# Retention scores: the sixteen-key tile with high and low keys in one 48-column stationary block

## The reference

```python
q, k = rotary(h @ w_q), rotary(h @ w_k) / sqrt(256)      # 4 heads, 256 wide each
s[i, j] = (q[i] . k[j]) * gamma_h ** abs(i - j)          # 272 x 272 for each head
o = s @ v                                                # v is 512 wide for each head
y = silu(g) * group_norm(o);   out = y @ w_out
```

## Time and profile before

| | us |
|---|---|
| median of 3 runs | 708.54 |
| the profiled execution, device time | 708.62 |
| its span in the trace | 706.8 |
| PE busy | 697.6 (99% of the span) |
| DVE busy | 610.9 (86%) |
| ACT busy | 518.0 (73%) |

### The profile page before, as it was taken

How to read it: one execution, slowest core, us unless ns; L and a number is a source line. 1 busy time by engine, 2 the same in 40 slices (tenths; PEclk the granted TensorE clock), 3 DMA queues, 4 the chain that set the end, 5 groups by cost and what they waited for, 6 DMA issues and landing times.

```text
span 706.8 us, 15923 instructions
## 1 busy us (share of the span) xinstructions
PE 697.6 (99%) x6495; PEld 585.3 (83%) x6495; DVE 610.9 (86%) x828; ACT 518.0 (73%) x834; POOL 28.0 (4%) x26
## 2 busy tenths in 40 slices
PE   9999999999999999999999999999999999999996
PEld 7888787887899888888889998888788888885464
DVE  6979897978789799989898879999999999999543
ACT  7477766757566888878787777999769888987431
POOL 0002020110100000000003100000000000000000
PEclk9999999999999999999999999999999999999999
DMA  9965646453481365644589941110625555565821
GB/s 342 315 250 149 240 140 249 131 180 141 180 312 55 136 217 190 227 178 178 186 314 391 368 173 61 61 60 1 234 84 218 194 223 203 213 237 205 261 42 60
DMA packets 47323, 134.31 MB, mean 190 GB/s; under 512 B 29728, under 2 KB 30240, under 8 KB 32032
## 3 DMA queue, kind: packets, MB, share of 16 engines
q1 hardware_dynamic: 46976, 133.20, 53.0%
q10 hardware_dynamic: 288, 0.31, 0.1%
HBM read 129.17 MB, written 1.05 MB: 184 GB/s over the span
## 4 chain that ended last, share of the span: by engine, by line
PE 89%; ACT 4%; DVE 4%; issue 1%; DMA 1%; DVEq 0%; ACTq 0%
PE ps L1658 23%; PE ps L1660 22%; PE ps L1659 22%; PE ps L2093 3%; PE ps L2095 3%; PE ps L2094 3%; PE ps L1701 2%; PE ps L1705 2%; PE ps L1700 2%; PE ps L1782 1%; PE ps L1779 1%; PE ps L1778 1%; PE ps L2033 1%; DMA hT<-in_tokens 1%; ACT work L846 1%
## 5 line engine op out<-in xcount | busy, mean ns | idle before, releaser
L1658 PE MATMUL ps<-a_hi,w_hi 128*128 128x272 f16 (+1 forms) x1000 | 277.1, 277 | 0.3 <-DVE work L1170 0.3
L1660 PE MATMUL ps<-a_hi,w_lo 128*128 128x272 f16 (+1 forms) x1000 | 277.1, 277 | 0.0
L1659 PE MATMUL ps<-a_lo,w_hi 128*128 128x272 f16 (+1 forms) x1000 | 277.1, 277 | 0.0
L1008 DVE SCALAR_TENSOR_TENSOR w_lo<-stage,w_hi 128x1024 f16<-128x1024 f32 x207 | 247.9, 1227 | 25.8 <-ACT w_hi L548 25.6
L548 ACT ACTIVATE w_hi<-stage 128x1024 f16<-128x1024 f32 x207 | 210.1, 1046 | 50.4 <-PE ps L1660 23.1
L1658 PEld LDWEIGHTS ps<-a_hi,w_hi 128*128 128x128 f16 x1000 | 97.8, 98 | 17.2 <-issue 0.7
L1660 PEld LDWEIGHTS ps<-a_hi,w_lo 128*128 128x128 f16 x1000 | 97.8, 98 | 16.0
L1659 PEld LDWEIGHTS ps<-a_lo,w_hi 128*128 128x128 f16 x1000 | 97.8, 98 | 15.8
L1658 PE MATMUL ps<-y_hi,w_hi 128*128 128x272 f16 (+3 forms) x496 | 106.2, 243 | 0.0
L1659 PE MATMUL ps<-y_lo,w_hi 128*128 128x272 f16 (+3 forms) x496 | 106.1, 243 | 0.0
L1660 PE MATMUL ps<-y_hi,w_lo 128*128 128x272 f16 (+3 forms) x496 | 106.0, 243 | 0.0
(11 more groups left out here) (281 smaller groups left out, 1089.3 us busy)
## 6 DMA issues: line engine op xcount, KB each, us to landing
stage<-in_chunks SPq DMA_DIRECT2D x118, 1024.0 KB
work<-work SPq DMA_DIRECT2D x96, 32.0 KB, 2.1
stage<-in_chunks SPq DMA_DIRECT2D x3, 512.0 KB
decay_all<-in_decay SPq DMA_DIRECT2D x1, 1056.0 KB, 13.7
out<-sq SPq DMA_DIRECT2D x4, 256.0 KB, 2.0
hT<-in_tokens SPq DMA_DIRECT2D x3, 272.0 KB, 6.2
stage<-in_chunks SPq DMA_DIRECT2D x2, 256.0 KB
mT<-in_gains SPq DMA_DIRECT2D x1, 512.0 KB, 6.4
```

What stands on the lines that cost most here:

```text
L1008: dve.scalar_tensor_tensor(out=part(1, c, q), in0=flat(stage, c, q), scalar=W_SCALE, in1=part(0, c, q), op0=ALU.mult, op1=ALU.subtract).th ...
L1658: pe.matmul(o, w_h, x_h, start=start, stop=False)
L1659: pe.matmul(o, w_h, x_l, start=False, stop=False)
L1660: return pe.matmul(o, w_l, x_h, start=False, stop=stop)
```

## The change

The two k-halves of the 16 small-tile keys get a stationary block of their own, `key_edge`, of 48 columns: columns 0 to 15 the high halves, 16 to 31 zeros, 32 to 47 the low halves. Two matmuls (moving: high queries, low queries) take the place of three. They leave in PSUM rows 0 to 15 the scores with the high keys and in rows 32 to 47 the scores with the low keys. These are not added: rows 32 to 47, times the decay, go to rows 96 to 111 (`R_KEY`) of the small tile of `s_hi`, a third copy of v_hi goes to the same rows of `v_hi`, and the P.V matmul L1931 runs over 112 rows where it ran over 80. The product of low keys and low queries is now included as well.

```diff
-        R_HI, R_LO = 32, 64
+        R_HI, R_LO, R_KEY = 32, 64, 96
+        key_edge = carve(R_HI + META).bitcast(F16).rearrange("p (k c) -> p k c", k=2)
...
                 def qk_high(x):
                     act.wait_ge(rot_done, 2 * h + x + 1)
+                    if (h, x) == (0, 0):
+                        act.wait_ge(zeroed, 1)
+                    act.activation(key_edge[:, x, 0:META], rotq[:, 2 + x, 2 * P:T], ACTF.Copy)
                     act.activation(halves(qk_hi, x), halves(rotq, x), ACTF.Copy).then_inc(qkhi_made, 1)
...
                     if n == 2:
-                        act.activation(v_hi4[R_HI:R_HI + m, n], vs[n][0:m], ACTF.Identity, bias=vsum[0:m, n, 1:2])
+                        for row in (R_HI, R_KEY):
+                            act.activation(v_hi4[row:row + m, n], vs[n][0:m], ACTF.Identity, bias=vsum[0:m, n, 1:2])
...
                 def qk_low(x):
                     dve.wait_ge(qkhi_made, 2 * h + x + 1)
+                    dve.tensor_tensor(key_edge[:, x, R_HI:], rotq[:, 2 + x, 2 * P:T], key_edge[:, x, 0:META],
+                                      ALU.subtract)
...
                 last.then_inc(s_dec, 1)
+                if h == 0:
+                    dve.wait_ge(zeroed, 3)
+                dve.tensor_tensor(s_hi[R_KEY:R_KEY + META, 2, :], ps[R_HI:R_HI + META, A + 2, 0:T],
+                                  decay_sb[R_HI:R_HI + META, h, R_HI:R_HI + T], ALU.mult)
...
+            pool.memset(key_edge[:], 0.0).then_inc(zeroed, 1)
             pool.memset(v_hi[:, 2, :], 0.0).then_inc(zeroed, 1)
...
-                    for n, (m0, m) in enumerate(TOK_TILES):
+                    for n, (m0, m) in enumerate(TOK_TILES[0:2]):
                         key = slice(m0, m0 + m)
-                        mm = three(ps[0:m, A + n, 0:T], qk_hi[:, 2 + k, key], qk_lo[:, 2 + k, key],
-                                   qk_hi[:, k, :], qk_lo[:, k, :], k == 0, k == 1)
+                        three(ps[0:m, A + n, 0:T], qk_hi[:, 2 + k, key], qk_lo[:, 2 + k, key],
+                              qk_hi[:, k, :], qk_lo[:, k, :], k == 0, k == 1)
+                    pe.matmul(ps[0:R_HI + META, A + 2, 0:T], key_edge[:, k, :], qk_hi[:, k, :],
+                              start=k == 0, stop=False)
+                    mm = pe.matmul(ps[0:R_HI + META, A + 2, 0:T], key_edge[:, k, :], qk_lo[:, k, :],
+                                   start=False, stop=k == 1)
                 mm.then_inc(s_up, 1)
...
-                    mm = pe.matmul(ps[:, A + e, 0:T], v_hi[0:R_LO + META, 2, col], s_hi[0:R_LO + META, 2, :],
+                    mm = pe.matmul(ps[:, A + e, 0:T], v_hi[0:R_KEY + META, 2, col], s_hi[0:R_KEY + META, 2, :],
                                    start=False, stop=True)
```

More of the change, by code:

```diff
@@ L723, in _ @@
                     if (h, n) == (0, 2):
-                        act.wait_ge(zeroed, 1)
+                        act.wait_ge(zeroed, 2)
                     if n == 2:
-                        act.activation(v_hi4[R_HI:R_HI + m, n], vs[n][0:m], ACTF.Identity, bias=vsum[0:m, n, 1:2])
+                        for row in (R_HI, R_KEY):
+                            act.activation(v_hi4[row:row + m, n], vs[n][0:m], ACTF.Identity, bias=vsum[0:m, n, 1:2])
                     act.activation(v_hi4[0:m, n], vs[n][0:m], ACTF.Identity,
@@ L735, in _ @@
                 if h == 0:
-                    act.wait_ge(zeroed, 2)
+                    act.wait_ge(zeroed, 3)
                 act.activation(s_hi[R_LO:R_LO + META, 2, :], sT[0:META, 2, :], ACTF.Copy)
```

## The result

The changed kernel takes 709.32 us (median of 22 runs, 708.93 to 709.73) against 708.48 us for the kernel before (22 runs beside it): +0.84 us, a ratio of 1.0013 (95% interval 1.0007 to 1.0019). It is slower, by less than the 0.2% that the prediction took as the limit of a change that counts. The forecast was +0.17 us. The time lies inside the stated range, but the change is five times the forecast one, and unlike it is clear of noise.

What follows compares the result with a forecast made beforehand. PE, busy 99%, was taken as the bound, with head 0's end set by the DVE and ACT path. 0.93 us saved against 1.09 of new waiting gave net +0.17, 708.7 us from a 708.54 median; range 707.1 to 709.4.

Steps and rivals of the forecast that it cites:

- The bound and its place: PE bounds the kernel; work added between head 0's scores and the transposes costs PE time one for one.
- PE, removed: Scores of each head: 8 fewer matmuls at 0.116 us each in all, 0.23 us less per head, 0.93 in all.
- Changing between block sizes: Around the small tile on PE: each change costs 0.10 us extra, at 48 columns as at 16; no difference taken.
- P.V over 112 rows, and the small operations ahead of the scores: P.V on PE, and copies and subtractions on ACT and DVE (together under 0.75 us, covered): no cost.
- DVE, the low keys' scores: Extra 16x272 product on DVE: 0.35 us (bounds 0.15 and 0.5), on the path in head 0.
- The same term in head 3: DVE's extra product in heads 1 to 3: costs nothing, ahead of 0.37 us of waiting for ACT.
- ACT, the third copy: Third copy of v_hi on ACT: +0.74 us on the path in head 0, nothing in heads 1 to 3.
- The sum: Whole kernel: 0.93 us saved on PE, 1.09 of new waiting in head 0, net +0.17 us.
- (b): Rival: all added work is hidden and PE sheds eight matmuls, -0.93 us, 707.6 us; chance 0.09.
- (c): Rival: the 48-column block needs no change of size on PE, -1.3 us, 707.2 us; chance 0.10.
- (d): Rival: added work also delays `v_out` in heads 1 and 2, 710.1 us; chance 0.06 including doubled block-change cost (710.3).
- The clock: Caveat: if the clock fell after head 0's 1.5 us wait, each such microsecond would cost another.

Runs made afterwards that it cites:

- the kernel with exchanged rows: Changed kernel with the small operands' rows exchanged, so DVE's low-key product reads and writes rows 32 to 47; 709.24 us against 708.47 for the kernel before, ratio 1.0011.

## Why the prediction was wrong, point by point

- **The bound and its place: right.** PE alone sets the time, and what is added between L1295 and the transposes of head 0 comes out of PE's time. Taking out the copy, the product or the wait for the means shortened the wait in head 0 by 0.73, 0.69 and 1.19 us, and the medians went down by 0.67, 0.71 and 0.98, the same within their intervals.
- **PE, removed: 0.93 forecast, 0.75 measured.** Eight matmuls went, but the 48-column block's inner step is 0.13 to 0.14, and head 1's next chunk began 0.07 us late (0.28 us from start to start).
- **Changing between block sizes: right**, 0.20 to 0.21 at 48 columns as at 16. The load that might have stood bare behind each change, by the estimate from the Trainium skill, "TensorE: Matmul & The Clock Gate", section LDWEIGHTS, does not show: the step into the block is 0.20, not longer than before. The profile gives the load 0.09 us at 16 columns and 0.10 at 48, not 13 and 40 ns; the measurement decides. Whether the wider load is behind the longer inner step, no run shows. Padding the block to 128 columns makes the two steps plain, and is worth more than the change itself: 1.4 us (1.97 less 0.53) against 0.7.
- **P.V over 112 rows, and the small operations ahead of the scores: right.** The step behind L1947 is 0.12; the low halves are done at 37.78 us, 3.2 us before the scores.
- **DVE, the low keys' scores: the term that was mis-sized.** "Nearest row, same shape and same source: 0.35" took a row that begins at partition 0. In head 0 the product costs 0.56 where it stands and 0.11 more at the transposes, 0.67 in all. L1304, also 16x272 but written from partition 32 on, takes 0.46 from start to start and would have been nearer.
- **The same term in head 3: +0.23 in place of nothing.** The text set 0.35 against 0.37 us of idle time on DVE. The idle time is the same in head 3, but 0.56 does not fit into it, and the low half of the scores comes 0.23 later. That counts there because only 36 matmuls stand between the scores and P.V in place of 96, and DVE's last step had ended 0.15 us before P.V started; the text looked at the cover at `v_out` and not at `slo_made`. With the product at row 0, 0.35 us long, P.V of head 3 starts 0.16 behind its neighbour: at the forecast price the cover would have held.
- **ACT, the third copy: right in size**, 0.72 for 0.74. Overlooked was that it delays the gate's eviction (DVE's L1167) in head 1, which stands ahead of L1302 and releases PE's next chunk: the 0.07 us above. Without the copy they are gone.
- **The sum** is thereby off by 0.74 on the timelines: 0.21 for the product in head 0, 0.11 between the weights' low halves and the transposes, 0.02 for small steps, 0.17 for the smaller saving of PE, 0.23 in head 3.
- **The 0.11 us at the transposes, 13 us behind the product.** It appears in head 0 of all eight runs that have the product off row 0 and in none of the five without it, and never in heads 1 and 2. In head 0 nothing on DVE reads PSUM between the product and the transposes; in the other heads the group norm's root (L1020, `rs<-ps,rs`) does, from row 0. So the rows fit this: a DVE instruction does not start before its forerunner's end if it reads PSUM from other rows on than the last one that read PSUM did. That is an inference from these rows; no run puts it to the test by itself.
- **The rivals.** (b) is refuted by the wait that grew, (c) by the steps of 0.20 and 0.21 us, which stayed. (d) named delays that reach the wait for `v_out` in heads 1 and 2; these did not come (head 2's chunk follows P.V without a gap). What came was the same kind of thing at other semaphores, in head 3 and, by 0.07 us, in head 1.
- **Luck among the signs.** The transposes were to end near 59.4 us and end at 59.44. But the forecast put PE's start of the scores at 41.33, and it was 40.97 in this execution: 0.36 us of luck cancel the 0.34 us by which the way through head 0 is longer than forecast.
- **The clock** stayed at its full level: granted 1.00 from 55 to 60 us, where the 1.98 us lie, and behind them.

## What to carry to other kernels

When work is added to an engine that is nowhere the bound, list every semaphore the bounding engine waits on behind it, for each pass of the loop, the first and the last ones by themselves: the two large losses here (1.43 and 0.23 us) were in passes whose order differs from the middle ones. Saving two matmuls of six was worth 0.23 us a head at most; the four changes of block size around them cost 0.4, and padding the odd block with zeros to 128 columns takes them away. A saving on PE pays only after the chain beside it has been shortened: with three small instructions moved and the copy given to the idle engine, the same idea turned from +0.84 into -1.25 us, and with the padded block into -2.49. But compare with the old kernel under the same repairs: moving the three instructions gives it -0.53, and padded blocks on top -1.97. The merged products themselves are worth 0.5 to 0.7 us.

## What the runs showed of the hardware that was not expected

- DVE instructions in a row that begin at partition 0 start 0.06 to 0.1 us before the one ahead has ended. Three kinds did not and began 0.01 to 0.04 us behind it: one that reads and writes from partition 32 on (the product of the kernel with exchanged rows) and the one behind it; L1304, which reads from partition 0 and writes from 32; and, all at partition 0, one that reads what the one ahead wrote (L1014 to L1015). The same 16x272 product costs 0.35 us at partition 0 and 0.56 at 32; whether it wrote from 96 or from 32 on made no difference. No run reads from 32 and writes from 0, so which side does it in the product is open.
- A change between a 128-column stationary block and one of 16 or 48 columns makes the step 0.20 to 0.21 us in place of 0.116; zeros up to 128 columns take that away.
- POOL's copy of 16x512 16-bit elements took 0.73 us in head 0 and 1.12 in the others. What DVE did beside it in head 1 lasted no longer for it: the low half of the small value tile took 0.74 us and the gate's eviction 1.29, as in the kernel with the means first and the copy on ACT.
